# A bidirectional encoder trunk on one core: each weight block as three matmuls of 256 columns in place of one of 512 and one of 256

## The reference

```python
for i in range(DEPTH):                                  # DEPTH = 2
    shift, scale, gate = modulation(i, 0)               # cond @ ada_w + ada_b
    h = rms_norm(x, norm_g[i, 0]) * (1.0 + scale) + shift
    out = short_conv_mixer(h, ...) if i == 0 else mamba2_bidir_mixer(h, ...)
    x = x + gate * out
    shift, scale, gate = modulation(i, 1)
    h = rms_norm(x, norm_g[i, 1]) * (1.0 + scale) + shift
    x = x + gate * (jnp.square(jax.nn.relu(h @ mlp_w1[i])) @ mlp_w2[i])
return rms_norm(x, final_g)
```

## Time and profile before

| what | value |
|---|---|
| time, median of 2 runs | 2854.27 us (2852.66 to 2855.89) |
| the profiled execution's own time | 2845.86 us |
| its span in the profile | 2843.8 us |
| mean granted TensorE clock | 0.97 |
| PE matmuls busy | 2605.5 us, 92% of the span, 14828 instructions |
| PE weight loads busy | 2272.5 us, 80%, 14828 instructions |
| DVE busy | 2164.3 us, 76% |
| ACT, POOL busy | 1355.9 us (48%), 1035.3 us (36%) |
| mean busy share of the DMA engines, by stage | 0.53 to 0.89 |

### The profile page before, as it was taken

The page is one execution under the profiler, slowest core; times in us unless marked ns, Lnnn a source line. Parts: engine busy times, 40 slices in busy tenths (PEclk is TensorE's granted clock), DMA queues, the critical chain, the costliest instruction groups (busy, mean ns, idle before and its releaser), DMA issues.

```text
span 2843.8 us, 46780 instructions
## 1 busy us (share of the span) xinstructions
PE 2605.5 (92%) x14828; PEld 2272.5 (80%) x14828; DVE 2164.3 (76%) x2499; ACT 1355.9 (48%) x2022; POOL 1035.3 (36%) x917
## 2 busy tenths in 40 slices
PE   0399998999999999979999999999879999999997
PEld 0288887888888888868888888888768888888886
DVE  6988889986877779887888878888775555555555
ACT  2244444544444444454555545555454444444443
POOL 3522235442333334534555424555551111112123
PEclk9999999999999999989999999999899999999999
DMA  8899889786877788846656576555545555555553
GB/s 328 310 322 319 310 326 348 266 311 228 277 292 276 277 307 326 325 168 207 206 202 206 200 274 212 186 201 209 190 147 189 188 184 189 185 185 185 185 184 133
DMA packets 171667, 679.62 MB, mean 239 GB/s; under 512 B 18672, under 2 KB 35312, under 8 KB 146704
## 3 DMA queue, kind: packets, MB, share of 16 engines
q1 hardware_dynamic: 171488, 677.75, 68.3%
q0 software_dynamic: 48, 0.13, 0.0%
HBM read 675.58 MB, written 2.23 MB: 238 GB/s over the span
## 4 chain that ended last, share of the span: by engine, by line
PE 70%; DVE 12%; issue 7%; POOL 3%; ACT 2%; DVEq 0%; ACTq 0%; POOLq 0%
PE psm L874 44%; PE psm L876 22%; DVE wl L1054 3%; DVE adat L1067 3%; PE psy L981 2%; ACT wh L662 1%; POOL xd L556 1%; POOL ss L477 1%; POOL x L602 1%; DVE normt L1340 1%; PE psm L892 0%; POOL x L503 0%; DVE dec L1293 0%; DVE rbc L1256 0%; DVE normt L1293 0%
## 5 line engine op out<-in xcount | busy, mean ns | idle before, releaser
L1054 DVE TENSOR_TENSOR wl<-raw,wh 128x1024 fp32r<-128x1024 f32 x862 | 1175.3, 1364 | 413.6 <-ACT wh L662 408.7
L874 PE MATMUL psm<-hcat,wh 128*128 128x512 f32 x3984 | 1414.6, 400 | 7.5 <-DVE tt L1084 4.8
L876 PE MATMUL psm<-hcat,wl 128*128 128x256 f32 x3984 | 1117.9, 281 | 0.0
L662 ACT ACTIVATE wh<-raw 128x1024 fp32r<-128x1024 f32 x866 | 912.2, 1053 | 206.9 <-PE psm L876 142.6
L874 PE MATMUL psm<-hid,wh 128*128 128x512 f32 x2560 | 901.0, 397 | 6.3 <-POOL hid L573 5.3
L874 PEld LDWEIGHTS psm<-hcat,wh 128*128 128x128 f32 x3984 | 754.6, 189 | 187.8 <-DVE wl L1054 6.1
L876 PEld LDWEIGHTS psm<-hcat,wl 128*128 128x128 f32 x3984 | 757.4, 190 | 0.2
L876 PE MATMUL psm<-hid,wl 128*128 128x256 f32 x2560 | 717.6, 280 | 0.0
L874 PEld LDWEIGHTS psm<-hid,wh 128*128 128x128 f32 x2560 | 481.6, 188 | 122.9 <-POOL hid L573 5.6
L876 PEld LDWEIGHTS psm<-hid,wl 128*128 128x128 f32 x2560 | 484.3, 189 | 0.0
L1067 DVE CUSTOM_DVE_ANT_0 adat<-adat,cond 128x2048 f32<-128x2048 f32 x176 | 434.9, 2471 | 14.2 <-DMA adat<-in_ada 14.1
(11 more groups left out here) (157 smaller groups left out, 1959.0 us busy)
## 6 DMA issues: line engine op xcount, KB each, us to landing
raw<-in_w SPq DMA_DIRECT2D x866, 512.0 KB, 4.1
adat<-in_ada SPq DMA_DIRECT2D x176, 1024.0 KB, 5.6
xs<-in_ada SPq DMA_DIRECT2D x8, 1024.0 KB, 7.1
zs<-in_ada SPq DMA_DIRECT2D x8, 1024.0 KB, 6.2
normt<-running_sums SPq DMA_DIRECT2D x32, 256.0 KB, 4.8
dec<-running_sums SPq DMA_DIRECT2D x32, 256.0 KB, 5.6
x<-in_xT SPq DMA_DIRECT2D x1, 2048.0 KB, 17.1
out<-x SPq DMA_DIRECT2D x4, 512.0 KB, 2.6
```

The lines of the kernel that those rows point to most:

```text
L662: act.activation(wh[:, h % 4, :], raw[:, h % 4, :], ACT.Copy).then_inc(hi_done, 1)
L874: pe.matmul(bank[:, :], wh[:, h % 4, k * P:(k + 1) * P], src[:, kb, :], start=(kb == 0), stop=(kb == KB - 1), skip_group_check=True)
L876: mm = pe.matmul(bank[:, T:2 * T], wl[:, h % 4, k * P:(k + 1) * P], src[:, kb, 0:T], start=False, stop=(kb == KB - 1), skip_group_check=True)
L1054: dve.tensor_tensor(wl[:, h % 4, :], raw[:, h % 4, :], wh[:, h % 4, :].bitcast(F32), ALU.subtract).then_inc(lo_done, 1)
```

## The change

The matmul of 512 columns is written as two of 256, with the same weights: first the high columns of the activations into columns 0 to 255 of the bank, then the low columns into columns 256 to 511. The second no longer has the flag `start`, since the flag of the first one already resets the whole bank. The third matmul, with `wl`, stays as it was. The change is in `unit` and in `pair`, not in `half_outs`. No wait, buffer, transfer or other engine's instruction is touched. All lines behind the change move by 2 or 4.

```diff
@@ unit @@
-                        pe.matmul(bank[:, :], wh[:, h % 4, k * P:(k + 1) * P], src[:, kb, :],
+                        pe.matmul(bank[:, 0:T], wh[:, h % 4, k * P:(k + 1) * P], src[:, kb, 0:T],
                                   start=(kb == 0), stop=(kb == KB - 1), skip_group_check=True)
+                        pe.matmul(bank[:, T:2 * T], wh[:, h % 4, k * P:(k + 1) * P], src[:, kb, T:2 * T],
+                                  start=False, stop=(kb == KB - 1), skip_group_check=True)
                         mm = pe.matmul(bank[:, T:2 * T], wl[:, h % 4, k * P:(k + 1) * P], src[:, kb, 0:T],
                                        start=False, stop=(kb == KB - 1), skip_group_check=True)
@@ pair @@
-                        pe.matmul(bank[:, :], wh[:, h % 4, k * P:(k + 1) * P], hcat[:, kb, :],
+                        pe.matmul(bank[:, 0:T], wh[:, h % 4, k * P:(k + 1) * P], hcat[:, kb, 0:T],
                                   start=(kb == 0), stop=(kb == KB - 1), skip_group_check=True)
+                        pe.matmul(bank[:, T:2 * T], wh[:, h % 4, k * P:(k + 1) * P], hcat[:, kb, T:2 * T],
+                                  start=False, stop=(kb == KB - 1), skip_group_check=True)
```

## The result

The kernel with three matmuls a block takes 2900.53 us (median of 2 runs, 2897.26 to 2903.79), against 2854.27 before: a ratio of 1.0176, 95% interval 1.013 to 1.0221, 46 us slower. The profiled execution has a span of 2895.2 us, 51.4 more than before, at a granted clock of 0.972 (0.97 before).

The account below looks back on a forecast made before the run. PE's cost per block was taken to bound the kernel: 1558 us removed, 1555 added, so -3 us, giving 2843 from the profiled 2845.9. Against the runs' median it forecast 2854 us, no change; 8 in 10 range 2785 to 2940.

Parts of the forecast that it names:

- What bounds the kernel: PE sets the pace; what a block of weights costs on PE, 0.350 us, is paid nearly block for block.
- The count: Each of 6672 blocks swaps one 512-column step for two of 256; same columns, three loads for two, no wait added.
- rival D: The second matmul with the same weights goes without a load; time within a few us of forecast, sharing its 0.70.
- So the added steps look like the one that is there, load included: On PE, each added 256-column step costs today's 0.1165 us with its load; 1555 us added in all.
- 0.360, +67 us: Upper bound: every PE step at 0.12 us makes a block 0.360 us, adding 67 us.
- The added load is hidden beneath columns, with 5 ns to spare: On PE, loads need 0.110 to 0.112 us a step, just below the 0.1165 us of a 256-column step.
- Rival A: Every matmul or load on PE has a fixed 13 to 17 ns; adds 87 to 113 us, about 2950; chance 0.17.
- Rival B: Short PE steps run at the load's pace, 0.112 to 0.113 us; 80 us less, about 2775; chance 0.10.
- Rival C: Loads on PE can't overlap, three of 0.19 us make 0.57 us a block; some 4300 us; chance 0.03.
- The cover: At 400 to 500 us DVE has the least room, so a faster PE would gain little there; no size given.

Follow-up runs that it names:

- runs 2 and 5: Kernel before with both matmuls at 512 columns: 3443.59 us; the same with each of them split into two of 256: 3626.13 us.
- Run 4: Changed kernel with weights of 64 columns in place of 128 in all three matmuls: 2822.33 us.
- runs 12 to 15: Weights of 64 columns in the kernel before, in two matmuls of 512, four of 256, two of 384: 2804.16, 3478.55, 3463.74, 2834.76 us.
- run 8: Changed kernel with 192 streamed columns in each of the three matmuls, whole loads: 2791.85 us.
- run 3: Kernel before with both matmuls of a block at 384 columns: 2835.62 us.
- run 11: Changed kernel with the long matmul split into 384 and 128 columns in place of 256 and 256: 3181.95 us.
- runs 9 and 10: Kernel before, matmuls reordered over two blocks: wh, wh, wl, wl, 2846.36 us, ratio 0.9997; wh, wl, wl, wh, 2846.41 us, ratio 0.9993.

## Why the prediction was wrong

It said no change, 2854 us; measured are 2900.5, and the slowdown of 46 us is clear of the noise (at least 1.3% by the interval). The time lies inside the stated range and within 2% of before.

- **What bounds the kernel** was right: PE's steps, block for block. In the stretches with PE busy throughout the difference of the blocks is the difference of the starts.
- **The count** was right, and with it rival D fell: 6672 more matmuls and as many more loads, no wait added in the program, DVE's work unchanged (2164.3 and 2166.1 us), the half clock free of the surplus, 0.64 us a block.
- **The step that failed** is "So the added steps look like the one that is there, load included", with its 0.1165 us. That step was read from a stream in which every short step has a long one beside it. The reading was right: by the starts in the trace of the kernel before, the short steps have a mean of 0.115 us and the long ones 0.232 from 1000 to 1200 us, and 0.117 and 0.236 from 2200 to 2800. But among equal steps the short one is 0.120 and the long one 0.227 (the changed kernel, runs 2 and 5). In the mixed stream a part of the surplus of the short matmul sits on the step of the long one: 0.115 + 0.232 is 0.347, as is 0.120 + 0.227. The change took the long step out at its full 0.232 or 0.236 and put short ones in at 0.1165 that only that neighbour allowed. The term was three times 3.5 ns a block too low, 0.3495 instead of 0.360. Both ends of it were on paper, and the upper one, "0.360, +67 us", is what a block takes; the middle was taken for no better reason than that the means of the rows lay there.
- **"The added load is hidden beneath columns, with 5 ns to spare"** was the sentence to distrust. The text went on that if the cover failed, all three steps would pay. They do, 3.5 ns each. Run 4 shows that the width of the weights has a part in it: halve it and the step falls to 0.113 in most of the program. It doesn't show why whole loads, which under 192 columns follow each other every 0.112 us, take 0.120 under 256.
- **Rival A**, a fixed cost of matmul or load, 17%, had the sign and about the size: it asked for 13 to 17 ns a block. The blocks paid 13.3 where they ran at 0.346 before, and 6.7 where they ran at 0.353. Its argument against itself, that 0.230 and 0.1165 aren't equal shares, rested on a mixed stream; in equal streams the surplus is the same 32 cycles for 256, 384 and 512 columns. As a fixed cost it is no mechanism either (runs 12 to 15), but as a sum, the surplus of a whole block over the number of its matmuls, it gave 13 ns and was the better forecast. Its 87 to 113 us are times of 2941 to 2967, so all of A lay above the stated 2940, not its upper half.
- **Rival B**, a pace under 0.342, fell: equal steps don't run at the pace of the load, they run above it. **Rival C** fell, loads overlap. The Trainium skill, page Perfetto Trace Analysis, section Identifying the Most-Contended Engine, takes the busy share of weight loads for a measure of how near TensorE is to its limit. By that rule the trace disagrees: in the stretches above the share went to 100%, with a load every 0.120 us, while run 8 starts one every 0.112.
- **The cover**, price that waits take up, was named for 400 to 500 us only. Some 7 us of it are in the Mamba mixer, whose stretch paid 2.0 ns a block. With 67 us as the price of the blocks the total shows 46 to 51. That the time came out inside the range is owed in part to this and to the bound of +67, not to the forecast's mechanism.

What stays open: why a whole load under 256 columns makes 288 cycles and not 268, the pace of run 8; why weights of 32 columns are dearer than those of 64; why run 4 has both 0.113 and 0.120 with the same instructions; and what sets a mixed stream to 832 or 848 cycles a block.

## What to carry to other kernels

Read the price of a matmul from a stream of the same lengths as the one you are going to build: in a mixed stream a short step can leave part of its price on the long step beside it. Where only a mixed stream is at hand, share out the surplus of a whole block over its matmuls, here 26 ns over two at the faster pace. Before you split a matmul, remember that each piece brings a load along: here a split into 256 and 256 columns costs up to 13 ns, and an uneven one (384 and 128) 60. And where a cost has two bounds, a term with 6672 instances deserves more than the middle.

## What the runs showed of the hardware

- In fp32r streams with whole loads and equal matmuls at the full clock, a matmul of 256, 384 or 512 columns takes 32 cycles more than its columns (0.120, 0.1733, 0.2267 us: the changed kernel, runs 3 and 2). At the half clock 256 and 512 columns take 0.21 and 0.43 us, their columns alone.
- The closest starts of whole loads in these streams are 0.11 us apart (0.112 in run 8, 0.11 in run 11), and a piece of 128 columns makes its neighbour pay (run 11: 0.17 us for 256 columns).
- A stream that alternates 512 and 256 columns has two rhythms, 0.3467 and 0.3533 us a block, and stayed in one for 600 us (2200 to 2800). In two other orders (runs 9 and 10) the same matmuls held 0.348. Equal steps of 384, with the same number of columns and loads, held 0.3467; they took 2835.62 us in one run, 16 under the median of before and 6 under its fastest of 13, which one run doesn't settle, and run 3 leaves out part of the products.
- The same instructions can have two paces in equal streams too: run 4, with weights of 64 columns, had steps of 0.113 and, for some 350 us, of 0.120.
